# Gate rows spread over the partitions from a scratch in HBM, asked for earlier, and two PSUM banks exchanged

## What is computed

```python
def token_mixers(p, pc, b_gate, norm_g, rpb, cos, sin, rows, need_ctx):
    qm, km, vm, om, qn, kn, vn, gm = jnp.split(p, cuts, axis=-1)       # pc likewise, for the context
    y_m, yc_m = mlstm_group(qm, km, vm, om, gm, ...)                   # both directions, then a head norm, times sigmoid(om)
    y_n, yc_n = neighborhood_attention(qn, kn, vn, qnc, knc, vnc, ...) # softmax over a window and the context
    return jnp.concatenate([y_m, y_n], axis=-1), ...

# mlstm_scan, one chunk
b = jnp.cumsum(fc, axis=-1)                                            # sums of the log forget gates
d_intra = jnp.where(causal, b[..., :, None] - b[..., None, :] + ic[..., None, :], -jnp.inf)
w_intra = jnp.exp(d_intra - m_t[..., None])
s = jnp.einsum('bhtd,bhsd->bhts', qc, kc) * w_intra
```

## Time and profile before

| | |
|---|---|
| median of 3 runs | 3657.22 us (3654.48 to 3663.42) |
| profiled execution | 3656.94 us, its span 3655.2 us, granted PE clock 0.971 |
| PE busy | 3405.2 us (93%) |
| DVE busy | 1352.2 us (37%) |
| ACT busy | 677.3 us (19%) |
| `pairs` in layer 2 | from 2250 to 2611 us of the span |
| `pairs` in layer 3 | from 3131 to 3392 us of the span |
| transfers of gate rows (L627) | 32 of 256 KB, 26.2 us from issue to landing |

### The profile page before, as it was taken

How to read it: one execution, slowest core, us unless ns; L and a number is a source line. 1 busy time by engine, 2 the same in 40 slices (tenths; PEclk the granted TensorE clock), 3 DMA queues, 4 the chain that set the end, 5 groups by cost and what they waited for, 6 DMA issues and landing times.

```text
span 3655.2 us, 43237 instructions
## 1 busy us (share of the span) xinstructions
PE 3405.2 (93%) x16156; PEld 2534.0 (69%) x16156; DVE 1352.2 (37%) x3259; ACT 677.3 (19%) x1440; POOL 41.1 (1%) x80
## 2 busy tenths in 40 slices
PE   7999999989999999999999999777999999867999
PEld 4888854556888888886658884333488885434888
DVE  3444523324444554453331011333354454234100
ACT  2000022432000010002441012333310002333100
POOL 0000000000000000000000000000000000000000
PEclk8999999989999999999999999888999999988999
DMA  5443232633222232224465456444132225664443
GB/s 222 160 161 134 88 108 69 219 132 117 87 90 84 81 127 90 84 87 147 169 245 180 154 168 122 43 48 32 35 134 86 87 87 134 82 64 44 167 150 109
DMA packets 114545, 422.43 MB, mean 116 GB/s; under 512 B 12864, under 2 KB 16064, under 8 KB 112352
## 3 DMA queue, kind: packets, MB, share of 16 engines
q1 hardware_dynamic: 104256, 376.49, 29.5%
q0 software_dynamic: 7776, 40.77, 10.0%
q10 hardware_dynamic: 2368, 3.10, 0.2%
HBM read 410.87 MB, written 1.05 MB: 113 GB/s over the span
## 4 chain that ended last, share of the span: by engine, by line
PE 83%; DMA 8%; DVE 3%; ACT 3%; issue 2%; POOL 0%; SPq 0%; DVEq 0%; ACTq 0%
PE PS L806 27%; PE PS L858 16%; PE PS L739 11%; PE PS L919 7%; DMA mix<-arena 6%; PE PS L1173 3%; PE PS L1164 3%; PE PS L879 2%; PE PS L661 2%; DMA ring<-stream 2%; PE PS L1009 2%; PE PS L722 1%; PE PS L1091 1%; PE PS L1074 1%; PE PS L708 1%
## 5 line engine op out<-in xcount | busy, mean ns | idle before, releaser
L739 PE MATMUL PS<-xn,ring 128*128 128x256 f32 (+1 forms) x1664 | 422.2, 415 | 6.1 <-DMA ring<-stream 3.2
L739 PEld LDWEIGHTS PS<-xn,ring 128*128 128x128 f32 x1664 | 314.7, 190 | 107.7 <-issue 65.4
L806 PE MATMUL PS<-xn,ring 128*128 128x256 f32 x1312 | 301.9, 384 | 4.5 <-DMA ring<-stream 2.4
L806 PEld LDWEIGHTS PS<-xn,ring 128*128 128x128 f32 x1312 | 248.8, 191 | 57.8 <-issue 19.1
L1173 PE MATMUL PS<-xn,arena 128*128 128x512 f32 (+1 forms) x640 | 274.4, 556 | 5.3 <-ACT mix L1647 3.9
L919 PE MATMUL PS<-arena,ring 128*128 (+2 forms) x1120 | 273.8, 407 | 1.6 <-DVE arena L1863 1.6
L919 PEld LDWEIGHTS PS<-arena,ring 128*128 128x128 f32 x1120 | 214.6, 192 | 59.9 <-issue 33.9
L858 PE MATMUL PS<-xn,ring 128*128 128x256 f32 x752 | 223.6, 379 | 0.0
L858 PE MATMUL PS<-arena,ring 128*128 128x256 f32 x784 | 202.1, 380 | 0.3
L858 PE MATMUL PS<-xn 128*128 128x256 f32 x752 | 193.0, 379 | 0.0
L1438 ACT ACTIVATE arena<-PS 128x256 f32<-128x256 f32 x82 | 31.0, 382 | 815.5 <-PE PS L806 815.5
(11 more groups left out here) (264 smaller groups left out, 4248.1 us busy)
## 6 DMA issues: line engine op xcount, KB each, us to landing
ring<-stream SPq DMA_DIRECT2D x716, 512.0 KB, 3.4
arena<-pair_m POOLq DMA_DIRECT2D x8, 1536.0 KB, 7.1
arena<-pair_n POOLq DMA_DIRECT2D x8, 1024.0 KB, 5.3
mix<-arena POOLq DMA_DIRECT2D x32, 256.0 KB, 26.2
mix<-head_w POOLq DMA_DIRECT2D x16, 320.0 KB, 3.3
mix<-na_bias POOLq DMA_DIRECT2D x8, 512.0 KB, 3.9
h<-xT ACTq DMA_DIRECT2D x1, 1024.0 KB, 21.2
h<-ctxT ACTq DMA_DIRECT2D x1, 1024.0 KB, 33.0
```

The lines of the kernel that those rows point to most:

```text
L739: m = pe.matmul(PS[:, bank, 0:tokens], ring[:, s, k * P:(k + 1) * P], xn[:, k, 0:tokens], start=k == 0, stop=k == DC - 1)
L806: m = pe.matmul(out, weights, moving, start=k == 0, stop=k == 3)
```

## The change

There are four parts. A scratch `gate_sums` of 64 x 512 floats is made in HBM; once per layer Pool writes `g_a` into it (128 KB) and waits for that, and the four spreads of a pair read a row of it instead of a partition of SBUF. For pairs 1 to 3 these spreads are issued before the wait on `na_acc` and before pair_n, for pair 0 after pair_n as before, with the write to the scratch ahead of pair_n. `own_weights(i + 1, 0)` and `(i + 1, 1)` are called at n = per - 3 and per - 2: 5 and 6 in layer 2, and as before 1 and 2 in layer 3. And nq goes to bank 3 and nk to bank 2, with the wait for the sigmoid copy moved from the first product of nq to the first of nk.

```diff
--- before.py
+++ after.py
@@ -418,6 +418,7 @@
         pm_arow = [sem(f"pm_arow{e}") for e in range(2)]
         pm_score = sem("pm_score")
         pm_ltri = sem("pm_ltri")
+        sums_out = sem("sums_out")
         pm_w = sem("pm_w")
         pm_p = sem("pm_p")
         pm_turned = sem("pm_turned")
@@ -569,6 +570,7 @@
         def last_down(ph):
             return [q for q in PLAN[:PLAN.index(ph)] if q.kind in ("down", "down7", "mix2")][-1]
 
+        gate_sums = nc.dram_tensor("gate_sums", (64, TOK), F32, kind="Internal").ap()
         block = ctx.enter_context(nc.Block())
 
 
@@ -624,19 +626,25 @@
                             pool.wait_ge(pm_w, i * per + N0 - 1 + e)
                         for d in range(2):
                             row = 32 * d + 2 * i + e
-                            pool.dma_start(arows[e][d], g_a[row:row + 1, :].rearrange("p (o n) -> p o n", o=1).broadcast_to([1, P, TOK]))\
+                            pool.dma_start(arows[e][d], gate_sums[row:row + 1, :].broadcast_to([P, TOK]))\
                                 .then_inc(pm_arow[e], 16)
                     for i in range(HP):
                         pool.wait_ge(pm_acc, i * 3 + (3 * Q0 + CREDIT))
                         pool.dma_start(pairw[:, 0:3, :].rearrange("p j n -> p (j n)"),
                                        pair_m[bass.ds(i + Q0, 1)].rearrange("o p n -> p (o n)")).then_inc(pairm_in, 16)
+                        if i == 0:
+                            pool.wait_ge(gate_rows, ph.at.gates)
+                            pool.dma_start(gate_sums, g_a).then_inc(sums_out, 16)
+                            pool.wait_ge(sums_out, 16 * ph.at.gates)
+                        else:
+                            arow(i, 0)
+                            arow(i, 1)
                         pool.wait_ge(na_acc, i * 2 + (2 * Q0 + CREDIT))
                         pool.dma_start(pairw[:, 3:5, :].rearrange("p j n -> p (j n)"),
                                        pair_n[bass.ds(i + Q0, 1)].rearrange("o p n -> p (o n)")).then_inc(pairn_in, 16)
                         if i == 0:
-                            pool.wait_ge(gate_rows, ph.at.gates)
-                        arow(i, 0)
-                        arow(i, 1)
+                            arow(i, 0)
+                            arow(i, 1)
                         pool.wait_ge(pair_done, i + (Q0 + CREDIT))
                         pool.dma_start(nabias.rearrange("p a b n -> p (a b n)"),
                                        na_bias[bass.ds(i + Q0, 1)].rearrange("o p n -> p (o n)")).then_inc(bias_in, 16)
@@ -1199,8 +1207,9 @@
                     j, k = x // DC, x % DC
                     if x == 0:
                         pe.wait_ge(pairn_in, p * 16 + 16 * (Q + 1))
+                    if x == DC:
                         pe.wait_ge(pm_copied, p * 3 + (3 * Q + 3))
-                    m = pair_product(ph, j, k, 2 + j, TOK if j else ph.tokens, 3 + j)
+                    m = pair_product(ph, j, k, 3 - j, TOK if j else ph.tokens, 3 + j)
                     if k == DC - 1:
                         m.then_inc(na_acc, 1)
 
@@ -1650,7 +1659,7 @@
                 def neighbour_copy(p, j):
                     act.wait_ge(na_acc, p * 2 + (2 * Q0 + j + 1 + CREDIT))
                     n = TOK if j else T
-                    act.activation(qkna[:, j, 0:n], PS[:, 2 + j, 0:n], ACT.Copy, scale=1.0 if j else float(HD) ** -0.5)\
+                    act.activation(qkna[:, j, 0:n], PS[:, 3 - j, 0:n], ACT.Copy, scale=1.0 if j else float(HD) ** -0.5)\
                         .then_inc(na_copied, 1)
 
                 for j in range(3):
@@ -2327,8 +2336,8 @@
                             dve.wait_ge(pm_std, i + (Q0 + 1))
                             link(dve.reciprocal(small[:, 24:24 + per], small[:, 16:16 + per]))
                             tt(mtok, mtok, wide(small[:, 24:24 + per]), ALU.mult).then_inc(pm_normed, 1)
-                        if not last and n in (1, 2):
-                            own_weights(i + 1, n - 1)
+                        if not last and n >= per - 3 and n < per - 1:
+                            own_weights(i + 1, n - (per - 3))
                         if not last and n == spot_of(ROTATE_AT, per) // 2:
                             rope(i + 1)
                     dve.wait_ge(na_exp, i * per + (N0 + per))
```

## The result

The changed kernel takes 3502.94 us (median of four runs, 3501.51 to 3503.71) against 3657.2 us (3654.48 to 3663.42): a ratio of 0.9575, with a 95% interval of 0.9559 to 0.9592. On two more occasions it took 3497.73 and 3496.47 us. The forecast was 3497.

The account below looks back on a forecast made before the run. It took TensorE, stalled behind VectorE's waits for slow one-partition spreads, as the bound. Savings of 84.9 (layer 2), 73.5 (layer 3) and 2 us (scores) make 160.4; 3656.9 less that is 3496.5, forecast 3497 us, range 3485 to 3560.

Parts of the forecast that it names:

- The bound and the culprit: In `pairs`, VectorE's `own_weights` waits 179.8 us for slow spreads of one SBUF partition, and TensorE idles behind it.
- Layer 2, 28.3 us per iteration: Second halves in layer 2: PE's idle time and low-clock slowness vanish, 61.7 to 33.4 us; 84.9 us for three iterations.
- Layer 3, 24.5 us and the 0.7 us of scores: Layer 3: of 29.9 us a 5.2 us chain stays, 73.5 us saved in three iterations; faster opening scores add 2 us.
- the cover in layer 3: Time from asking for the spreads to their use in layer 3: 19 to 21 us, against 13 us for four spreads.
- Work costed at nothing: Scratch fill (at most 3.3 us a layer), moved `own_weights`, pair_n queued later, Pool's descriptor writing: all hidden, 0 us.
- The banks: First neighbour product skips a 1.31 us wait, PE may wait for probabilities instead: 0 to 1.3 us per iteration, taken as 0.
- Rival A: One HBM row serves no better than one partition, 38 us for four spreads: 3552 us, up to 3606 if worse; 20%.
- B: Repeated reads of one HBM row are slower still, over 55 us for four: slower than before, 3816 us at twice today's; 5%.
- C: ACT and DVE chains leave gaps in the shortened second halves, 2 us for each of six: 3509 to 3517 us; 10%.
- D: The wait does not hold the end, since PE was the bound anyway: 3657 us; 1%.

Follow-up runs that it names:

- hbm_only: The kernel before with the HBM scratch as the spreads' source; asking, use and banks as before: 3497.82 us, ratio 0.9561.
- sbuf_distinct2: The kernel before with each spread replaced by a copy of 128 different rows, one from each SBUF partition of xn; gate sums left out of the weights: 3498.26 us.
- hbm_only_again: The kernel before with only the spreads' source changed to the HBM scratch, run once more on another occasion: 3500.68 us, ratio 0.9568.
- after_again: The changed kernel, unaltered, run once more on one chip with three other kernels: 3497.73 us, ratio 0.9565.
- after_third: The changed kernel, unaltered, run a third time, beside a variant on the same chip: 3496.47 us, ratio 0.9562.
- products_first: The changed kernel with one more neighbour product ahead of an iteration's first turning and none in the thirteenth place: 3500.94 us, ratio 0.9563.
- sbuf_in_after: The changed kernel with one SBUF partition as the spreads' source again and no scratch: 3564.71 us, ratio 0.9746.

## Why the prediction was right

**The bound and the culprit** (one partition as the source, seen in the comparison of landings): shown, by hbm_only and by sbuf_distinct2, which leave the asking, the use and the banks in place.

**Layer 2, 28.3 us per iteration.** Measured by the distance between the issues of pair_m or the bias, before less after: 27.3, 28.7 and 29.1, together 85.1 against 84.9. The second half became 33.07 us, forecast 33.4.

**Layer 3, 24.5 us and the 0.7 us of scores.** Measured 24.5, 24.8 and 25.6, together 74.9 against 75.5. The second half became 21.85 us (3137.22 to 3159.07 in PE's timeline), forecast near 22. Both layers: 160.0 us against 160.4. The granted clock returned with the work, as the sum had it: six products of 128x512 take 2.74 us in each of these halves. But the step that gave 24.5 had luck in it. It took the end of a layer 3 iteration as a chain through VectorE of 5.2 us; in after it takes 5.5 us, and PE does not idle in it (21.84 us busy of 21.85). VectorE's last reciprocal of the chain, then PE's twelve products in the same time and the sums behind them:

```profile
3157.39 0.17 DVE L2344 RECIPROCAL small<-small 128x4 f32<-128x4 f32 x1
```

```profile
3154.87 2.75 PE L1181 MATMUL PS<-xn,arena 128*128 128x256 f32 x12
3157.61 0.66 PE L1284 MATMUL PS<-cst,small 128*64 128x128 f32 x8
```

The products, which the sum left out, and the chain end within 0.1 us of each other. The 0.7 us for the scores was low by its own rows (2.08 less 1.13 is 0.95), and the cover in layer 3 was too wide: asked for 3.7 us later, the second pair of rows has some 18 us, not 19 to 21. Neither changed the outcome.

**Work costed at nothing.** The scratch holds Pool for 1.97 us once a layer, behind which pair_n and the spreads stand, all in time (bound 3.3 us). The moved `own_weights` and pair_n's later place in the queue: nothing, as hbm_only_again beside after_again shows. The banks: nothing, with the exchange of waits that was named.

**The last 6 us of the first comparison.** 160 us were saved in `pairs`, but the spans differ by 153.2 (3655.2 less 3502.0). The rest lies outside, in code that is the same in both: after reaches its first pair_m 9.0 us later and 2.1 us are won back between and behind the loops. Most of the 9.0 lies between the last transfer of head_w and that of the masks: 325.7 us in before and 332.8, 328.5 and 326.8 in after, after_again and after_third. The window 1880 to 1960, first of before, then of after, after_again and after_third, with the granted clock in the third column from the end:

```profile
1880.00:1960.00 80.00, 70.96 (x410) 52.63 (x410) 19.31 (x46) 24.54 (x53) 0.00 (x0) 0.96 0.53 191
```

```profile
1880.00:1960.00 80.00, 70.21 (x379) 51.68 (x379) 19.88 (x49) 24.48 (x52) 0.00 (x0) 0.85 0.48 172
```

```profile
1880.00:1960.00 80.00, 69.97 (x396) 51.88 (x395) 19.09 (x46) 24.85 (x53) 0.00 (x0) 0.91 0.51 185
```

```profile
1880.00:1960.00 80.00, 69.99 (x407) 51.99 (x406) 19.32 (x46) 24.56 (x53) 0.00 (x0) 0.96 0.51 188
```

The first pair_m is asked for at 2195.9 us in before and at 2204.8, 2199.0 and 2196.7 in the three others: the delay goes with the clock of this stretch, not with the change. In after_third, where that clock was 0.96 as in before, the span was 3494.0 us, 161.2 less. It does not settle the whole span: hbm_only had 0.89 here and a span of 3493.6 us, products_first 0.96 and 3498.1. Why this stretch is granted more or less of the clock from one execution to the next stays open.

**Rival A's mechanism, now measured.** sbuf_in_after is A as it was told: forecast 5.3 us lost in a layer 2 iteration and 13.1 in layer 3, measured 8.0 (70.6 less 62.6) and 13.5 (55.4 less 41.9), 3564.7 us for 3552. The second pair landed 40.2 us after the first asking, as told (40). What A's sum lacked in layer 2 is the low clock behind the remaining idle time, though the forecast counted it elsewhere: sums and values took 2.8 us (2417.2 to 2420.0) for its 1.5.

```profile
2417.23 1.97 PE L1280 MATMUL PS<-cst,small 128*64 128x128 f32 x16 [5.96 <-DVE small L2340]
```

That the earlier asking and later use would keep most of the gain holds, 94 of some 160 us. What did not come is the slow HBM row, at 38 to 47 us for four. The Trainium skill ("SBUF — State Buffer", section "A bandwidth-pool intuition that's wrong (but worth ruling out)") gives about 22.5 GB/s for a port of the HBM crossbar, which would be, as an estimate, 11.7 us for 256 KB if a row lay behind one port; the slowest spread of after took 9.8 us and the median 4.3, so a repeated row was not held to one such port here.
B fell with it; its price for twice today's rate, 16 and 28 us, should have been 15 and 27 by its own numbers (76 less 61 and 49), some 7 us less in all. Of C, the feared gaps did not appear: PE is busy 32.96 of 33.07 us. The likely reason: the halves that prepare a next pair put six products behind each of the first two turnings, where the last one, from which C was argued, has four and two instructions and waits 2.67 us next. D is out with the gain.

## What to carry to other kernels

When a transfer is slow, compare its landing with others of the same queue, size and number of rows written: here that named the source, and the source was worth everything (3497.8 us by itself), while asking sooner and using later only hid part of it. Where something waits for it, don't spread one SBUF partition over all the others by DMA; put the rows into HBM once and read them from there (26.2 us became 4.3 here). And a wait that is taken off an engine with another wait right behind it, like the banks here, is worth at most the difference of the two, not its own length.

## What was not expected of the hardware

One partition as the source held sixteen DMA engines to 27 GB/s, while one HBM row read as often landed at 4.3 us per 256 KB (61 GB/s each, with other spreads beside it), only 1.2 us behind 128 different rows (3.1 us). A reciprocal on VectorE of 128x512 took 3.35 us where an addition or a product of two tiles of that size takes 0.69. And the granted clock of the same untouched 80 us was 0.85, 0.91 and 0.96 in three executions of the same program.
